# Giving the weight ring back one slot at a time, and moving two product tiles ahead of a group norm

## The reference, cut to what matters

```
p = h @ w_in;  u, q, k, v, zr, gl = split(p)
y_a = multiscale_pool(u)
y_b = diff_attention(q, k, v)
y_c = rwkv7_bidir(zr)      # recurrence, forward and backward, 8 heads of 64
merged = sum_n sigmoid(gate_n) * (y_n @ w_branch_n);  x = layer_norm(alpha*x + merged @ w_out)
x = layer_norm(alpha*x + relu(x @ w_up)^2 @ w_down)
```

```
y = direction(0, forward) + direction(1, reverse)
mu = mean(y);  var = mean((y - mu)^2);  y = (y - mu) * rsqrt(var + eps) * gn_g + gn_b
y_c = (y + bonus) * gate
```

## Time and profile before

| | |
|---|---|
| time, 3 runs | median 3922.16 us, 3920.52 to 3924.79 |
| the profiled execution | 3922.59 us, span 3920.8 us |
| PE, PEld | 3759.4 us (96%), 3041.0 us (78%) |
| DVE, ACT, POOL | 43%, 37%, 35% |
| recurrence, layer 0 / layer 1 | some 122 to 372 us / 1248 to 1498 us |
| load of one unit (2 MB), median | 7.7 us |
| DMA queue of the kind "instruction" | 232 packets, 3.80 MB, 0.4% of the 16 engines' time |

### The profile page before, as it was taken

One profiled execution on the slowest core, in us unless ns is written; L12 is line 12 of the kernel. 1 busy time (PEld: TensorE's weight loads), 2 busy tenths in 40 slices (PEclk: granted clock), 3 DMA queues, 4 the chain that ended last, 5 costly groups with the idle time before them and its releaser, 6 DMA issues.

```text
span 3920.8 us, 67096 instructions
## 1 busy us (share of the span) xinstructions
PE 3759.4 (96%) x28976; PEld 3041.0 (78%) x28976; DVE 1679.8 (43%) x2714; ACT 1438.2 (37%) x2442; POOL 1382.9 (35%) x581
## 2 busy tenths in 40 slices
PE   8888999999999899999999999999999999999999
PEld 7677768888887776687888876778888777788887
DVE  6554441487145554612683167415111376332112
ACT  3354252323233443522223243634222436434222
POOL 5000324444442002144444454233444353244443
PEclk9999999999999999999999999999999999999999
DMA  3001212266221001132473221112222221122222
GB/s 145 2 4 46 83 60 102 86 248 231 86 89 42 4 4 66 68 113 86 161 274 133 93 101 65 44 65 102 90 104 86 105 89 34 63 98 86 86 108 86
DMA packets 37150, 356.65 MB, mean 91 GB/s; under 512 B 4224, under 2 KB 4352, under 8 KB 17920
## 3 DMA queue, kind: packets, MB, share of 16 engines
q1 hardware_dynamic: 19584, 278.93, 19.3%
q10 hardware_dynamic: 17280, 73.48, 5.2%
HBM read 350.29 MB, written 2.10 MB: 90 GB/s over the span
## 4 chain that ended last, share of the span: by engine, by line
PE 84%; DVE 7%; ACT 3%; issue 2%; DMA 1%; POOL 1%; PEld 1%; PEldq 0%; DVEq 0%; SPq 0%; ACTq 0%; POOLq 0%
PE banks L762 23%; PE banks L764 23%; PE banks L763 23%; PE banks L1121 10%; PE banks L2166 3%; ACT arena L2319 1%; DMA ring<-stream 1%; ACT arena L1484 1%; PE banks L2248 1%; DVE arena L1964 1%; PE banks L1230 1%; DVE arena L1858 0%; DVE x L2706 0%; POOL ring_r L860 0%; PE banks L1436 0%
## 5 line engine op out<-in xcount | busy, mean ns | idle before, releaser
L860 POOL TENSOR_TENSOR ring_r<-ring,hi_ring 128x1024 fp32r<-128x1024 f32 x490 | 1201.6, 2456 | 2206.9 <-ACT hi_ring L851 2206.6
L762 PE MATMUL banks<-xT_r,ring_r 128*128 128x512 f32 (+1 forms) x2480 | 953.8, 385 | 13.4 <-POOL ring_r L860 6.9
L764 PE MATMUL banks<-xT_r,hi_ring 128*128 128x512 f32 x2096 | 828.4, 395 | 0.0
L763 PE MATMUL banks<-x_lo_r,hi_ring 128*128 128x512 f32 x2096 | 824.1, 393 | 0.0
L851 ACT ACTIVATE hi_ring<-ring 128x1024 fp32r<-128x1024 f32 x490 | 511.2, 1046 | 731.8 <-DMA ring<-stream 301.0
L762 PEld LDWEIGHTS banks<-xT_r,ring_r 128*128 128x128 f32 x2480 | 470.4, 190 | 109.6 <-issue 15.9
L764 PEld LDWEIGHTS banks<-xT_r,hi_ring 128*128 128x128 f32 x2096 | 395.6, 189 | 94.2
L763 PEld LDWEIGHTS banks<-x_lo_r,hi_ring 128*128 128x128 f32 x2096 | 397.7, 190 | 89.9 <-issue 3.4
L1121 PE MATMUL banks<-arena 64*64 64x64 f32 (+4 forms) x7456 | 351.5, 248 | 53.3 <-DVE arena L1858 23.8
L1484 ACT ACTIVATE arena<-banks 128x512 f32<-128x512 f32 x366 | 214.7, 595 | 404.7 <-PE banks L764 242.8
L764 PE MATMUL banks<-hi_ring,pairs 128*128 128x512 f32 x864 | 342.3, 396 | 0.0
(11 more groups left out here) (263 smaller groups left out, 5462.8 us busy)
## 6 DMA issues: line engine op xcount, KB each, us to landing
ring<-stream SPq DMA_DIRECT2D x132, 2048.0 KB, 7.7
arena<-ada ACTq DMA_DIRECT2D x96, 512.0 KB, 4.7
arena<-ln_rows ACTq DMA_DIRECT2D x5, 1024.0 KB, 8.2
arena<-edge ACTq DMA_DIRECT2D x4, 1024.0 KB, 5.0
arena<-edge ACTq DMA_DIRECT2D x2, 1792.0 KB, 8.3
arena<-pack ACTq DMA_DIRECT2D x2, 1485.0 KB, 6.8
arena<-pack ACTq DMA_DIRECT2D x2, 1200.5 KB, 5.5
x<-x_in SPq DMA_DIRECT2D x4, 512.0 KB, 7.3
```

The lines of the kernel that those rows point to most:

```text
L762: first = nc.tensor.matmul(out_, left[1], right[0], start=start, stop=False)
L763: low = nc.tensor.matmul(out_, left[0], right[1], start=False, stop=False)
L764: return first, low, nc.tensor.matmul(out_, left[0], right[0], start=False, stop=stop)
L860: nc.gpsimd.tensor_tensor(feed.raw(n, ring_r), feed.raw(n), feed.hi(n).bitcast(F32), ALU.subtract).then_inc(split_lo, 1)
```

## The change

Each direction's `GM` (3072 columns) and `WU` (1024) now lie together in one ring slot: direction 0 in the slot that unit 4 will take, direction 1 in that of unit 5. `ring_back` stands behind link 6 of the last two groups (g = 6 is the last of direction 0, g = 7 of direction 1), and adds one to `weights_used` each time. `u 0` stands ahead of the `gn_mean` steps, `u 1` between them and `gn`; `gn_turn` and the first two `gn_out` move back by one tile. The floor of piece 15's split is now the step link 5 of the last group; pieces 16 on have the floor `u 0`.

```diff
-    if g == GROUPS - 1:
-        out[-2].append(("ring_back", ()))
+    if g >= GROUPS - 2:
+        out[-2].append(("ring_back", g % 2, ()))
...
+    add("u", 0, banks=(4,))
     for j in range(PAIRS):
         add("gn_mean", j, banks=(j % 2,))
+    add("u", 1, banks=(5,))
     add("gn", banks=(0,))
-    behind = {("u", 1): [("gn_turn",)], ("u", 2): [("gn_out", 0)], ("u", 3): [("gn_out", 1)], ("q", 1): [("gn_out", 2)],
+    behind = {("u", 2): [("gn_turn",)], ("u", 3): [("gn_out", 0)], ("q", 0): [("gn_out", 1)], ("q", 1): [("gn_out", 2)],
               ("q", 3): [("gn_out", 3)],
...
     for name in "uqk":
         for i in range(4):
-            add(name, i, banks=(4 + i % 2,))
+            if (name, i) not in (("u", 0), ("u", 1)):
+                add(name, i, banks=(4 + i % 2,))
...
-    out = with_splits(out, first_pieces(), {ZT: ("u", 0), UP_PIECE + HEAD: ("turn", 0, 3)},
+    out = with_splits(out, first_pieces(), {ZT: ("link", GROUPS - 1, 5), ZT + 1: ("u", 0), UP_PIECE + HEAD: ("turn", 0, 3)},
...
-    GM = [ring[:, 3072 * d:3072 * d + 3072].rearrange("p (q e b a t) -> p q e b a t", q=4, e=2, b=2, a=3) for d in range(2)]
-    WU = [ring[:, 6144 + 1024 * d:7168 + 1024 * d].rearrange("p (q e a t) -> p q e a t", q=4, e=2, a=2) for d in range(2)]
+    def in_ring(layer):
+
+        at_ = [UNIT * ((layer * UNITS1 + 4 + d) % RING) for d in range(2)]
+        return ([ring[:, a_:a_ + 3072].rearrange("p (q e b a t) -> p q e b a t", q=4, e=2, b=2, a=3) for a_ in at_],
+                [ring[:, a_ + 3072:a_ + 4096].rearrange("p (q e a t) -> p q e a t", q=4, e=2, a=2) for a_ in at_])
...
-                pe.drain().then_inc(weights_used, RING)
+                pe.drain().then_inc(weights_used, 1)
```

More of the change, by code:

```diff
@@ L1117, in first_tensor @@
         feed = feed1[layer]
+        GM, WU = in_ring(layer)
         seen = {}
```

## The result

The changed kernel takes 3934.45 us (median of 8 runs, 3929.57 to 3945.19) against 3918.12 of the kernel before in the same session (8 runs, 3912.98 to 3924.79). The ratio is 1.0047 with a 95% interval of 1.0035 to 1.0059: slower, outside the range and on the side of rival (c), which I had given 0.05. Engines are as busy as before; PE's own busy time is 3759.5 us instead of 3759.4. So look for idle time, first where (c) said. SP's timeline after: the load of unit 4 is issued at 357.98, where it used to start at 372.20 (the row merges the loads of units 4 and 5).

A forecast was written before the change was run, and what follows sets the result against it. PE, 96% busy, bounds the kernel; only its idle time and slow clock can be won: 10.45 - 2 x (0.5 + 1.2 + 1.2) - 1.75 = 2.9 us, so 3922.16 - 2.9 = 3919.3 us, range 3914 to 3925.

The forecast's parts named there:

- rival (c): Recurrence, 354 to 362 in layer 0: load starves PE's instruction supply, net 3.8 us worse per layer, 3929.8; chance 0.05.
- The load now runs beside the recurrence, where none ran before. I take nothing for that: Unit 4's early load: no cost; 1.6 us per layer if it doubles PE's existing 1.60 us stall.
- 2.3 us of gain per layer: Gain at the handover to the u tiles, set against 6.1 us of added stall per layer.
- the product tiles' loads: Argument against starvation: product tiles run beside such loads all the time with PE 96% busy, though issuing far fewer instructions.
- `u 0` now follows the links almost at once: At u 0, behind the links: clock still full, so 1.63 and 1.89 us are won.
- The clock at `gn`: Stretch between u 1 and u 2: clock falls in one of two layers, -1.75 us (bounds 0 and -3.5).
- (b): Clock falls at gn in both layers, so the gain is 1.15 us: 3921.0; chance 0.20.
- its three small waits: Per layer: 0.5 us at link 5, 1.2 ahead of u 0, 1.2 ahead of gn.
- link 5 late: ACT's split of piece 15 ahead of link 5 delays it and all behind by 0.5 us (bounds 0 and 1.05).
- the wait ahead of `u 0`: PE idle between the links and u 0, waiting for POOL's split: 1.2 us (bounds 0.6 and 2.0).
- the one ahead of `gn`: PE waits behind u 1 for ACT's copy and first square: 1.2 us (bounds 0.6 and 2.3).
- a fetch waits for little: DMA engines alternate between queues packet by packet, so an instruction fetch beside the load would hardly wait; no size given.

The follow-up runs named there:

- experiment 1: Kernel before plus only an unread 2 MB load, issued by ACT behind link 6 of group 6 in each layer: 1.0040, 3933.71 us.
- experiment 3: Kernel before with the change's layout and two returns, but the old order of u and the group norm: 1.0036, 3931.49 us.
- 2: Kernel before with only the new places of GM and WU, both slots given back together, old order: 1.0000, 3919.56 us.
- Experiment 9: The whole change, but direction 0's slot given back behind product wu of the last group: 1.0012 of the kernel before, 3924.54 us.
- experiments 6: Kernel before with the change's layout, old order and split place, direction 0's slot given back behind link 0 of the last group: 0.9993, 3917.99 us.
- 12: Old order with the layout and direction 0's slot given back behind link 0 of the last group, measured once more: 0.9990, 3915.57 us.
- Experiment 10: Kernel before plus an unread 2 MB load behind link 6 of group 6, in rows of 1 KB: 1.0014.

## Why the prediction was wrong, step by step

*"The load now runs beside the recurrence, where none ran before. I take nothing for that"*: this step failed. I had the stall in a row, 1.60 us with no visible cause, and bounded it by doubling. It tripled in layer 0 and grew more than fourfold in layer 1: +3.22 and +3.87 us, and the stretch behind it, at a low clock, +2.89 and +1.21. Experiments 1 and 3 show the load as cause, 2 clears the layout, 9 gives back most of it by moving the return. Rival (c) had the place, and a criterion that held ("issue" above 3.9 us; 4.82 and 5.01). Its sum did not hold. The stall was priced too high, 6.1 us more per layer where 3.2 and 3.9 were measured, since PE did not wait for the landing (365.50, with the load's last row still under way until 366.25). Its net, 3.8 us, was too low against the table's 7.8 and 7.4: it left out the clock, and kept 2.3 us of gain per layer that did not come. Against (c) I had put the product tiles' loads, where few instructions are issued; the gap between the fetches, which a view of the queues shows, bears on it more directly.

*"`u 0` now follows the links almost at once ... I take its 1.63 and 1.89 us as won"*: failed as well. `u 0` took 392.44 - 384.19 = 8.25 and 1520.30 - 1513.24 = 7.06 us, against 5.54 at full clock (and 7.17 and 7.43 before), so next to nothing was won. Experiment 9, with short stalls, has 7.27 (the next row starts at 381.07). In the change the clock is at 1.00 through the links (373 to 383) and at 0.55 in the 1 us behind them, so it falls as the links end, in the idle time ahead of `u 0`; in the kernel before, the links run straight into `gn_mean` and it stays up. Whether the waits between the links or the idle 1.19 us brings it down, no run separates.

*The clock at `gn`*: I took one layer of two. `u 2` was slow in both: 413.81 - 406.61 = 7.20 us, and 1543.28 - 1535.52 = 7.76 in layer 1; that is (b)'s term, 1.7 and 2.2 us where 1.75 in all was taken.

So the early return brought the loss, and the order, on which the gain rested, brought none: its three small waits came as forecast, the clock that was to pay for them didn't. The one gain that is left, some 3 us in experiments 6 and 12, has the old order.

*Right to a tenth*: link 5 late by 0.42 us (0.5 said), the wait ahead of `u 0` 1.19 (1.2), the one ahead of `gn` 1.30 by ACT's square (1.2). ACT's timeline shows the split between the links:

```profile
380.41 0.32 ACT L1492 ACTIVATE arena<-banks,small 128x64 f32<-128x64 f32 x1 [0.43 <-PE banks L1128]
380.62 1.05 ACT L854 ACTIVATE hi_ring<-ring 128x1024 fp32r<-128x1024 f32 x1
381.57 0.31 ACT L1492 ACTIVATE arena<-banks,small 128x64 f32<-128x64 f32 x1
```

The wait of 1.19 is labelled "issue", but POOL's half of the split ends at 384.10 and PE starts at 384.19: such a label can stand for an engine that ended last. The 4.82 has no such neighbour.

*Open*: why the clock after a stall is low for 27 us in one layer (experiment 1, layer 1) and for some 3 in another (experiment 3); and whether the unit itself, loaded early in small rows, would win, which wasn't tried.

## What to carry to other kernels

PE's instructions came here in fetches of 16 KB that the queue table lists beside the loads. Before moving a load beside a stretch with many small matmuls, compare the fetches in that table with it, and take an "issue" stall that is already there as a sign that there is no reserve. The same load 13 us further on, beside the links and `gn_mean`, was free. And price a stall with the clock behind it: in the profiled execution that was another 1.2 to 2.9 us per layer, and it varies from one execution to the next.

## What the runs showed of the hardware

Beside the products, a 2 MB load in rows of 4 to 16 KB delays the fetch of instructions by some 3 us (gaps of 8.0 to 8.7 instead of 5.1 to 5.4); in rows of 1 KB the gaps are 6.3 and 6.8. The Trainium skill (DMA: Bandwidth & Descriptors, "Queues, rings and completion order") has a DMA engine change queues only at the end of a packet, and a packet there is a run of descriptors, 9 to 17 as a rule (the profile's packets here are single rows, 75 for 1.23 MB). In the prediction I took from it that a fetch waits for little; that was my step and not the page's. Experiment 10 fits the rule, experiment 1 shows that the wait isn't little.

In the last two groups PE also stalls for 1.60 and 1.14 us with no load at all, likewise 1.2 to 1.6 us behind the end of a fetch. The Trainium skill (Runtime: NRT & Kernel Launch, "Instruction fetch mechanics") calls the cost of a new block of instructions mostly hidden; these stalls are not hidden.

Once the clock is down, the small matmuls of the recurrence don't always bring it back: 0.51 and 0.50 over 1493 to 1520 in experiment 1, while the same work in the kernel before (1484 to 1506) ran at 1.00 throughout.
